# Sparse-attention scores on the upper and lower 64 rows of TensorE, head pairs in alternating banks

## What is computed

```python
# MLA: 4 heads, 96 channels each; causal
s = einsum('bqhd,bkhd->bhqk', q, k) * scale; p = softmax(where(kpos <= qpos, s, NEG)); o = p @ v

# NSA: 4 query heads of 64 channels, ONE key head shared by all four, three branches
s_c = einsum('bqhd,bnd->bhqn', qf, kc) * scale        # 15 compressed keys
o_c = (softmax(where(m_c, s_c, NEG)) * m_c) @ vc
s_s = einsum('bqhd,bqnkd->bhqnk', qf, ksg) * scale    # selected blocks (here: all causal ones)
s_w = einsum('bqhd,bkd->bhqk', qf, kwi) * scale       # window (here: the whole causal past)
out = g0 * o_c + g1 * softmax(s_s) @ vs + g2 * softmax(s_w) @ vw
```

## Time and profile before

| | before |
|---|---|
| runs | 1525.32 us median (1525.18, 1525.32, 1527.6) |
| profiled execution | 1527.13 us, span 1525.6 us |
| TensorE matmul busy | 1486.4 us (97%) |
| VectorE busy | 1218.5 us (80%) |
| ScalarE busy | 1007.4 us (66%) |
| GpSimd busy | 78.1 us (5%) |
| mean granted TensorE clock | 0.994 |
| attention rounds, layer 0 | from 81.5 us to about 126.5 us |
| attention rounds, layer 1 | from 464.2 us to about 509.3 us |

### The profile page before, as it was taken

The page is one execution under the profiler, slowest core; times in us unless marked ns, Lnnn a source line. Parts: engine busy times, 40 slices in busy tenths (PEclk is TensorE's granted clock), DMA queues, the critical chain, the costliest instruction groups (busy, mean ns, idle before and its releaser), DMA issues.

```text
span 1525.6 us, 20008 instructions
## 1 busy us (share of the span) xinstructions
PE 1486.4 (97%) x7379; PEld 1244.9 (82%) x7379; DVE 1218.5 (80%) x1275; ACT 1007.4 (66%) x932; POOL 78.1 (5%) x120
## 2 busy tenths in 40 slices
PE   8998999999999899999999999999999999999996
PEld 6987888888898788878888888888888888888885
DVE  6778644544667879998899889888989899889986
ACT  6476544443547667777777777777777777777764
POOL 3101000000000010000000000000000000000000
PEclk9999999999999999999999999999999999999998
DMA  9705555555530269999999999999999999999991
GB/s 319 243 2 143 204 192 193 193 188 169 175 130 1 94 213 393 395 350 395 394 354 386 394 366 375 396 389 349 394 395 346 394 396 343 395 396 344 394 396 60
DMA packets 189820, 444.22 MB, mean 291 GB/s; under 512 B 9698, under 2 KB 15983, under 8 KB 189759
## 3 DMA queue, kind: packets, MB, share of 16 engines
q1 hardware_dynamic: 185206, 427.81, 76.4%
q0 software_dynamic: 4528, 15.58, 3.9%
q10 hardware_dynamic: 24, 0.01, 0.0%
HBM read 435.51 MB, written 7.86 MB: 291 GB/s over the span
## 4 chain that ended last, share of the span: by engine, by line
PE 91%; DVE 4%; ACT 3%; issue 1%; DMA 0%; SPq 0%; POOL 0%; POOLq 0%; DVEq 0%; ACTq 0%
PE bank L451 26%; PE bank L452 26%; PE bank L450 26%; PE bank L581 3%; PE bank L507 2%; PE bank L584 1%; PE bank L695 1%; DVE w_lo L1772 1%; PE bank L740 1%; DVE w_lo L1794 1%; ACT w_hi L1316 0%; PE bank L750 0%; PE bank L712 0%; PE bank L965 0%; PE bank L946 0%
## 5 line engine op out<-in xcount | busy, mean ns | idle before, releaser
L1794 DVE TENSOR_TENSOR w_lo<-ring,w_hi 128x2048 fp32r<-128x2048 f32 x372 | 846.5, 2290 | 176.3 <-ACT w_hi L1343 175.5
L1343 ACT ACTIVATE w_hi<-ring 128x2048 fp32r<-128x2048 f32 x372 | 712.1, 1917 | 223.0 <-PE bank L450 223.0
L451 PE MATMUL bank<-w_hi,xT_hi 128*128 128x512 f32 x896 | 353.5, 395 | 0.0
L452 PE MATMUL bank<-w_hi,xT_lo 128*128 128x512 f32 x896 | 349.4, 390 | 0.0
L450 PE MATMUL bank<-w_lo,xT_hi 128*128 128x512 f32 x896 | 240.2, 390 | 0.0
L451 PE MATMUL bank<-w_hi,hidT_hi 128*128 128x512 f32 x560 | 220.7, 394 | 2.8 <-DVE hidT_lo L1801 2.8
L452 PE MATMUL bank<-w_hi,hidT_lo 128*128 128x512 f32 x560 | 218.3, 390 | 0.0
L450 PEld LDWEIGHTS bank<-w_lo,xT_hi 128*128 128x128 f32 x896 | 168.1, 188 | 35.9 <-DVE w_lo L1772 0.2
L452 PEld LDWEIGHTS bank<-w_hi,xT_lo 128*128 128x128 f32 x896 | 168.3, 188 | 33.9
L451 PEld LDWEIGHTS bank<-w_hi,xT_hi 128*128 128x128 f32 x896 | 168.3, 188 | 33.7
L451 PE MATMUL bank<-w_hi,hT_hi 128*128 128x512 f32 (+2 forms) x384 | 148.1, 389 | 7.1 <-DVE hT_lo L1749 2.7
(11 more groups left out here) (379 smaller groups left out, 1269.5 us busy)
## 6 DMA issues: line engine op xcount, KB each, us to landing
ring<-in_moe_w_gate_dram SPq DMA_DIRECT2D x112, 1024.0 KB, 9.5
ring<-in_moe_w_up_dram SPq DMA_DIRECT2D x112, 1024.0 KB, 9.4
ring<-in_moe_w_down_dram SPq DMA_DIRECT2D x112, 1024.0 KB, 9.2
ring<-in_ffn_w_gate_dram SPq DMA_DIRECT2D x14, 1024.0 KB, 5.1
ring<-in_ffn_w_up_dram SPq DMA_DIRECT2D x14, 1024.0 KB, 5.1
ring<-in_ffn_w_down_dram SPq DMA_DIRECT2D x14, 1024.0 KB, 4.9
ring<-in_w_in_dram SPq DMA_DIRECT2D x12, 1024.0 KB, 6.4
ring<-in_w_out_dram SPq DMA_DIRECT2D x8, 1024.0 KB, 8.2
```

The source lines that it names most:

```text
L451: pe.matmul(o, x_hi, w, start=start, stop=False)
L452: return pe.matmul(o, x_lo, w, start=False, stop=False)
L1343: act.activation(w_hi[:, (base + at) % SPLIT, :], ring[:, i, :], ACT.Copy).then_inc(hi_ready, 1)
L1794: dve.tensor_tensor(w_lo[:, v, :], ring[:, (base + at) % RING, :], w_hi[:, v, :].bitcast(F32), ALU.subtract).then_inc(lo_ready, 1)
```

## The change

1. The NSA queries are transposed two heads at a time (128 channels at once): four transposes into one bank in the place of eight into two. ScalarE copies them in one instruction. Heads 0 and 2 now lie on partitions 0 to 63 of `nqT`, heads 1 and 3 on 64 to 127.
2. The key head is shared, so heads 1 and 3 need it on partitions 64 to 127 too: GpSimd issues two DMAs per layer, one that copies `kswT` (64 partitions x 2 KB) and one that copies `kcT` (64 x 60 bytes) from the lower to the upper half. TensorE waits for the first ahead of each sel score, and for both ahead of each cmp score (`keys_in`).
3. `scores(n)` takes all its banks first and then goes through the heads across the banks. For sel, win and cmp the heads 0 and 2 go to the first bank, 1 and 3 to the second, issued 0, 1, 2, 3; so successive matmuls use different halves of the rows and different banks. MLA's second step has heads 0 and 1 in the first bank, 2 and 3 in the second as before, but is issued 0, 2, 1, 3.
4. sel, win with 128 keys and both cmp steps now take two banks each in the place of one; VectorE reads them in the order of `heads_of`. Four more banks pass through the ring in each layer.

```diff
+        def heads_of(n):
+            br, tb = AJ[n]
+            if br == "mla":
+                return [[0, 1, 2, 3]] if tb == 0 else [[0, 1], [2, 3]]
+            return [[0, 2], [1, 3]]
...
                 pe.wait_ge(nsa_roped, l + 1)
+                b = bank(1)
                 for hp in range(2):
-                    b = bank(1)
-                    for i in range(2):
-                        c0 = O_NSA + (2 * hp + i) * HD
-                        for tb in range(TB):
-                            mm = pe.transpose(b[0:HD, (2 * i + tb) * P:(2 * i + tb + 1) * P],
-                                              utok[:, tb, c0:c0 + HD], ident[:, :])
-                    give(mm, 1)
+                    c0 = O_NSA + 2 * hp * HD
+                    for tb in range(TB):
+                        mm = pe.transpose(b[:, (2 * hp + tb) * P:(2 * hp + tb + 1) * P],
+                                          utok[:, tb, c0:c0 + 2 * HD], ident[:, :])
+                give(mm, 1)
...
                     if br == "cmp":
                         pe.wait_ge(dve_took, mark["cmp", l])
-                    per = 4 if br == "cmp" else 512 // nk
-                    for g in range(4 // per):
-                        b = bank(0)
-                        if n == 7:
-                            keep_busy(b, 2)
-                        for i in range(per):
-                            h = g * per + i
...
+                        pe.wait_ge(keys_in, 32 * (l + 1))
+                    elif br == "sel":
+                        pe.wait_ge(keys_in, 32 * l + 16)
+                    groups = heads_of(n)
+                    held = [bank(0) for _ in groups]
+                    if n == 7:
+                        keep_busy(held[0], 2)
+                    for i in range(len(groups[0])):
+                        for b, heads in zip(held, groups):
+                            h = heads[i]
+                            r = slice(h % 2 * HD, (h % 2 + 1) * HD)
+                            nq = nqT[r, h // 2, t0:t1]
+                            q, k = {"mla": (qT[0:QK, h, t0:t1], kT[0:QK, h, 0:nk]), "cmp": (nq, kcT[r, :]),
+                                    "sel": (nq, kswT[r, 0, 0:nk]), "win": (nq, kswT[r, 1, 0:nk])}[br]
                             mm = pe.matmul(b[:, i * nk:(i + 1) * nk], q, k, start=True, stop=True)
-                        give(mm, 0)
+                            if i == len(heads) - 1:
+                                give(mm, 0)
...
                 roots(4)
+                pool.wait_ge(act_took, mark["nsa", l])
+                pool.dma_start(kswT[HD:P, :, :], kswT[0:HD, :, :]).then_inc(keys_in, 16)
+                pool.wait_ge(dve_took, mark["cmp", l])
+                pool.dma_start(kcT[HD:P, :], kcT[0:HD, :]).then_inc(keys_in, 16)
                 roots(2, 0, False)
...
-                for hp in range(2):
-                    b = filled()
-                    act.activation(nqT[0:HD, 2 * hp:2 * hp + 2, :],
-                                   b[0:HD, :].rearrange("p (h t) -> p h t", h=2), ACT.Copy).then_inc(act_took, 1)
+                b = filled()
+                act.activation(nqT[:, :, :], b[:, :].rearrange("p (h t) -> p h t", h=2), ACT.Copy)\
+                    .then_inc(act_took, 1)
...
-                    per = 4 if br == "cmp" else 512 // nk
...
-                    for g in range(4 // per):
+                    for heads in heads_of(n):
                         b = filled()
-                        for i in range(per):
-                            h = g * per + i
+                        for i, h in enumerate(heads):
                             ins = dve.tensor_tensor_reduce(prob_of(n)[:, h, :], b[:, i * nk:(i + 1) * nk], m,
                                                            -scale, -NEG, ALU.add, ALU.min, rmin[:, n, h:h + 1])
                         empty_bank(ins)
```

More of the change, by code:

```diff
@@ L189, in trunk @@
                 at(b3, MLA_H, S), take(MLA_H, S),
-                at(b4, NH, S), take(2, S), take(NC), take(2 * HD), take(TB, SSD_H), take(4, HD),
+                at(b4, NH // 2, S), take(2, S), take(NC), take(2 * HD), take(TB, SSD_H), take(4, HD),
                 at(b5, CLEN // 2, 2, NC), take(TB, GW), take(TB, GW), take(SSD_H, P), at(used[0] - SSD_H * P, 2, S),
@@ L293, in trunk @@
         spread_ready = sem("spread_ready")
+        keys_in = sem("keys_in")
         cn_ready = sem("cn_ready")
@@ L683, in scores @@
                         pe.wait_ge(dve_took, mark["cmp", l])
-                    per = 4 if br == "cmp" else 512 // nk
-                    for g in range(4 // per):
-                        b = bank(0)
-                        if n == 7:
-                            keep_busy(b, 2)
-                        for i in range(per):
-                            h = g * per + i
-                            q, k = {"mla": (qT[0:QK, h, t0:t1], kT[0:QK, h, 0:nk]),
-                                    "cmp": (nqT[0:HD, h, t0:t1], kcT[0:HD, :]),
-                                    "sel": (nqT[0:HD, h, t0:t1], kswT[0:HD, 0, 0:nk]),
-                                    "win": (nqT[0:HD, h, t0:t1], kswT[0:HD, 1, 0:nk])}[br]
+                        pe.wait_ge(keys_in, 32 * (l + 1))
[12 more added lines that the diff above has]
+                                    "sel": (nq, kswT[r, 0, 0:nk]), "win": (nq, kswT[r, 1, 0:nk])}[br]
                             mm = pe.matmul(b[:, i * nk:(i + 1) * nk], q, k, start=True, stop=True)
-                        give(mm, 0)
+                            if i == len(heads) - 1:
+                                give(mm, 0)
                     mark["scores", l, n] = gave[0]
@@ L1211, in _ @@
             for l in range(L):
+                (qtok, kcat, vtok, xb, xbc, qT, kT, nqT, kswT, kcT, ckv, nacs, cvals, cin, xtok, xdt, dec1, kvT2,
+                 dec0) = mix_bufs[l]
                 roots(1, 0, False)
```

## The result

The changed kernel takes 1530.54 us, median of 15 runs (1528.9 to 1532.13), beside 1527.6 us for the kernel before (1525.18 to 1528.63, 15 runs). The ratio is 1.0023, 95% interval 1.0017 to 1.003. It is slower by some 3 us; the forecast was 1524.7, and the range ended at 1528.6. The forecast was counted from the median of three runs, 1525.32; with 15 runs the same kernel's median is 1527.6, so 2.3 us of the distance to the forecast lie in its base and not in the change. The profiled execution spans 1529.9 us (1525.6 before).

The account below looks back on a forecast made before the run. TensorE, holding 91% of the chain, was taken to bound the mixer, with ScalarE and the bank ring near-critical. Per layer -0.51 at the win scores, +0.90 ring, -0.68 win sum to -0.29, -0.6 for both: 1524.7 from 1525.32, range 1522.4 to 1528.6.

Parts of the forecast that it names:

- the clock falls: Rival: TensorE's wait ahead of the decay sums drops the clock, 1.7 us per fall; 1526.4 once, 1528.1 both; chance 0.20.
- MLA takes back 0.33: MLA's second step, issued 0, 2, 1, 3: takes back 0.33 of the transposes' 0.43 us on ScalarE's path.
- Sel's first step and `compress`, 0.5 gained: TensorE reaches `compress` at 87.05 in place of 87.55 us, 0.5 gained; the pairing there adds nothing more.
- Sel's second step -0.68: Sel's 256-column scores: row halves overlap, five slots in place of eight, 0.68 us less of TensorE.
- ScalarE gates the win scores: VectorE's win scores wait for ScalarE's copy of step 2's probabilities: begin at 100.80 against 101.31, 0.51 us gained.
- Bank ring +0.90: At the SSD decay sums: both pairs now wait for banks holding win scores, costing 0.90 us.
- Win's second step -0.68: Win's second scores: same saving as sel's, 0.68 us, all counted because TensorE carries the chain there.
- Cmp scores: nothing: Paired cmp scores lie beside the path over VectorE and ScalarE, so they gain or cost nothing.
- No overlap: Rival: row halves don't overlap, so win's second step saves nothing; +0.39 us per layer, 1526.1; chance 0.14.
- drains: Rival: each change of row half drains the array in sel's and win's steps; +4.0 us, 1529.3; chance 0.09.
- late keys: Rival: copied keys land 1.5 us late, ScalarE's chain slips 1.0; +2.4 us, 1527.7; chance 0.07.
- ScalarE not in the way: Rival: ScalarE's step 2 copies finish earlier, 1.18 us gained at win scores; -1.9 us, 1523.4; chance 0.08.

Follow-up runs that it names:

- e1: Changed kernel plus five filler matmuls (2.3 us) in TensorE's wait ahead of the decay sums; 1527.75 us, ratio to the kernel before 1.0001.
- e4: Kernel before with only the change's two-bank numbering for sel, win and cmp scores, all heads on the lower rows; 1533.08 us, ratio 1.0037.
- e9: Changed kernel run once more, unaltered, for a second profile; 1531.32 us in one run.
- e2: Changed kernel with MLA's second step issued head by head (0, 1, 2, 3) again; 1529.84 us, ratio to the kernel before 1.002.
- e8: e7 with four query transposes, a DMA copying heads 1 and 3 down, MLA in its old order; 1524.19 us, ratio to the kernel before 0.9979.
- e7: e3 plus filler matmuls ahead of the output projection; 1525.03 us, ratio to the kernel before 0.9989.
- e11: e1 with two filler matmuls (0.9 us) in place of five; 1529.12 us, ratio to the kernel before 1.001.
- e3: Kernel before with row pairs only in sel's and win's second steps (256 keys), which already used two banks; 1525.81 us, ratio 0.9991.
- e10: Kernel before run once more, unaltered, for a second profile; 1525.22 us in one run.

## Why the prediction was wrong

The step that failed is that the sum has no term for the clock: "the clock falls" stood beside it as a rival. The runs show in its place two falls in the decay sums, 1.57 and 2.57 us (e1 against after), and some 1 us more at layer 1's output projection, behind the paired cmp scores that the prediction put at nothing. The prediction names the place (the decay sums), the cause (a wait of some 2.8 us with little ahead of it) and the side, gives it 0.20, and calls 1.00 at 101 to 105 us the sign to look for. What spoke against it was one row, layer 0's stretch busy 2.14 of 5 us with no fall behind it. But rows 10 held one fall and one none at the same quiet; that is a coin, and here it was thrown twice with a longer wait (3.03 us beside 1.71). e4 shows such a coin: the same wait, a fall in one layer and none in the other. At 3 us every profile fell in both layers (after, e9 and, at 2.94, e2).

Its price was right for the one fall and too small for the other. I took 1.7 us from a stretch of projection, where the fall itself cost only 0.16. The decay sums are twelve float32 matmuls, 24 passes, back to back with nobody else to wait for. At 0.50 their passes stand 0.213 us apart and at 1.00 0.111, so each loses 0.10 us while the fall lasts: 1.57 and 2.57 us, in e4 2.81.

On the base of 15 runs the forecast of -0.6 would have read 1527.0, so 3.5 of the 5.8 us to 1530.54 are the change's and 2.3 the base's. The rival's "both", 1528.1, is +2.8 us on its base of 1525.32, and +2.9 was measured on 1527.6. That is luck. By the parts it is 4.1 us for the falls in the sums, 1.0 for the projection and twice -0.65 for the rest, +3.8; the 0.9 us between that and the measured +2.9 is no more than medians move by.

Point by point, on the scale of before:

- *Transposes -0.43:* right. The first scores stand at 82.96 - 1.92 = 81.04, predicted 81.05; alone (e8 against e7) -0.44.
- *MLA takes back 0.33:* right in kind; 0.26 at the decay sums in e2. The first row minimum stood at 87.18 - 1.92 = 85.26, predicted 85.29.
- *Sel's first step and `compress`, 0.5 gained:* 0.75; `compress` stands at 88.72 - 1.92 = 86.80 in place of 87.55.
- *Sel's second step -0.68:* the halves overlap more than that, 1.99 to 1.13, 0.86. I had weighed the Trainium skill's page TensorE: Matmul & The Clock Gate, "Part 3: Packing small matmuls", which says that such matmuls start about 4 ns apart and from which I estimated 0.91, and chosen the lower; the trace (0.86) is nearer to the page. Weight loads overlap as well: eight took 1.59 us and now 0.73. Products of step 1 at 93.49, predicted 93.9.
- *ScalarE gates the win scores:* right. Minima at 102.51 - 1.92 = 100.59 behind the copy, predicted 100.80. The copy itself gained 0.52 us (24.97 behind the transposes, 25.49 before), where I had 0.31.
- *Bank ring +0.90:* right, 0.92 in e4's layer 1. The wait ahead of the sums was 3.03 us. The Trainium skill's TensorEngine Tiling (Array Packing), "Gotcha 1: PSUM Pressure", says that row tiles write to different banks and so press on PSUM; the trace agrees, with this wait. By the clock the wait cost more than by itself: up to 2.57 us beside 0.92.
- *Win's second step -0.68:* -0.86.
- *Sum -0.29 per layer:* -0.65 with the clock held (e1). Of the difference, 0.18 is win's pair (0.86 in place of 0.68; sel's isn't on the path), and 0.21 the win scores, released at 100.59 in place of 100.80. The parts measured alone (0.92 - 1.05 - 0.44 + 0.26 = -0.31) leave 0.34 over. It lies in ScalarE's copy ahead of the win scores: 24.71 us behind the transposes in e2 and 25.05 in e8, both with four transposes and MLA's old order. Up to the copy, e2 differs by sel's pair of 128 keys and by the ring, and the ring alone leaves the copy where it was (25.48 in e4). That points at sel's first step in pairs, which no run has tried alone.
- *Cmp scores: nothing.* Wrong, by about 1 us in all. They end earlier and lengthen the next wait from 1.72 to 2.07 us, and the fall at layer 1's projection is long in all five profiles with paired cmp scores and no filler there. At layer 0's it is long in three of them (e9, e11, e1); of the unpaired ones only e3 falls there, for some 3 us and at no cost (350.24).
- *Keys: nothing.* Right; no wait for them, and the row of the profile's DMA issues has 2.2 us to landing for the 128 KB copies:

```profile
work<-work POOLq DMA_DIRECT2D x2, 128.0 KB, 2.2
```

- *No overlap; drains; late keys; ScalarE not in the way:* none came.

The later start. The query transposes stand at 76.26 to 76.94 us in five of the seven profiles of programs with four transposes, and at 75.02 to 75.43 in all seven others. The change touches nothing ahead of them. Part of it can be a wait for a load of the inputs (2.74 us in after, 1.56 in before), but e8 starts late with the shortest such wait, 1.37. What the five late profiles share is a late rise of the clock at the start of layer 0's input projection: of its first passes over 512 columns, 9 to 12 stand 0.43 us apart and the ones behind 0.23; in the nine other profiles at most 8 do. The same place in before and after:

```profile
15.38 0.39 PE L451 MATMUL bank<-w_hi,hT_hi 128*128 128x512 f32 x1
```

```profile
15.32 0.63 PE L459 MATMUL bank<-w_hi,hT_hi 128*128 128x512 f32 x1
```

Whether that goes with the programs is open; with so few profiles it may be chance, and if it isn't, the start is up to 1.9 us of the difference. e8, whose profile starts late, still has the best median.

## What to carry to other kernels

A change that speeds up work ahead of a wait makes TensorE quieter, and a quiet stretch is paid for by what stands behind it: read the wait and the busy share ahead of each back-to-back group, and if the wait there grows, put filler matmuls into it from the start, enough of them (2.3 us, which left 0.88 of the wait, held the clock here; 0.9 us, which left 2.16, didn't). When one row shows a fall at a certain quiet and another none, give the fall half the chance, and price it by the group that would be hit (here 0.10 us for each pass over 128 columns), not by the stretch where it was seen. Count a forecast from more than three runs of the kernel before: three were 2.3 us below fifteen here. Give row pairs only to the steps that use two banks anyway.

## What the hardware showed that I had not expected

- Matmuls on rows 0 to 63 and 64 to 127 overlap almost entirely, weight loads too: eight passes of 256 columns 1.99 to 1.13 us, of 128 columns 1.16 to 0.71. Same banks and order on one half: 1.99.
- The same program with the same 1.74 us wait ran its sums at 0.50 in one layer and at 1.00 in the other (e4).
- A fall isn't tied to the end of the wait: in e4 it came 0.9 us ahead of it, in layer 1 of e11 1.4 us behind it, in the middle of the sums.
- Filler cures the place where it stands and no other: e1 held the clock in the decay sums and fell at both projections.
- A short fall cost 0.1 to 0.16 us in layer 1's output projection, a long one 0.8 to 1.3; in the decay sums falls cost 1.6 to 2.8 us.
- The number of slow passes (0.43 us apart) at the start of layer 0's input projection is between 0 and 12 over the profiles, and 5 and 8 in two of the same kernel (before and e10).
